# Moving a tile of w_out between the inverse transforms, and the prompt's spectrum and the gating to GpSimd

## The reference

```python
def _mixer(h, rows, s0, l, p):
    proj = h @ p['w_in'][l]                       # q, ff, fb, iv, g, hy
    ...
    o_hg = o.reshape(B, L, HG_WIDTH) * jax.nn.silu(g)          # 512 channels: gated scans
    v, x1, x2 = jnp.split(hyc, [HY_WIDTH, 2 * HY_WIDTH], axis=-1)
    u = x1 * v
    z = _long_conv(u, kern) + p['hy_d'][l] * u                 # by Fourier transforms
    y_hy = x2 * z                                              # 512 channels: Hyena
    y_hy = y_hy * lax.rsqrt(jnp.mean(y_hy * y_hy, -1) + EPS) * p['hy_norm_w'][l]
    out = jnp.concatenate([o_hg, y_hy], -1) @ p['w_out'][l]

def _layer(x, cvec, rows, s0, l, p):
    sh1, sc1, g1, sh2, sc2, g2 = ...              # from the conditioning vector
    x = x + g1 * mixer(rmsnorm(x) * (1 + sc1) + sh1)
    x = x + g2 * convffn(rmsnorm(x) * (1 + sc2) + sh2)
```

## Time and profile before

| what | value |
| --- | --- |
| median of three runs | 913.55 us |
| the profiled execution | 912.88 us |
| its span | 911.1 us |
| VectorE busy | 717.0 us, 79% |
| ScalarE busy | 443.3 us, 49% |
| GpSimd busy | 38.9 us, 4% |
| chain that ended last, by engine | TensorE 84%, VectorE 9%, ScalarE 3% |
| TensorE's mean granted clock | 0.996 of full speed |

### The profile page before, as it was taken

How to read it: one execution, slowest core, us unless ns; L and a number is a source line. 1 busy time by engine, 2 the same in 40 slices (tenths; PEclk the granted TensorE clock), 3 DMA queues, 4 the chain that set the end, 5 groups by cost and what they waited for, 6 DMA issues and landing times.

```text
span 911.1 us, 14075 instructions
## 1 busy us (share of the span) xinstructions
PE 887.6 (97%) x5374; PEld 788.7 (87%) x5374; DVE 717.0 (79%) x911; ACT 443.3 (49%) x710; POOL 38.9 (4%) x58
## 2 busy tenths in 40 slices
PE   7999999999999999999899999999999999999997
PEld 4479898898898898688779999999999999998885
DVE  5744755966966985699678899999999999988645
ACT  5745324334343323332276756556565656565443
POOL 2200000100000000002000000000000000000000
PEclk9999999999999999999999999999999999999999
DMA  8765233144134244325511232233313232345703
GB/s 297 244 217 174 83 126 138 37 157 145 63 122 145 91 164 137 89 70 112 144 46 48 76 131 99 97 110 114 115 62 130 108 111 88 131 152 202 261 0 116
DMA packets 39275, 112.76 MB, mean 124 GB/s; under 512 B 4471, under 2 KB 12663, under 8 KB 38568
## 3 DMA queue, kind: packets, MB, share of 16 engines
q1 hardware_dynamic: 33944, 93.58, 30.3%
q0 software_dynamic: 4800, 17.99, 6.5%
q10 hardware_dynamic: 464, 0.30, 0.1%
HBM read 101.48 MB, written 10.37 MB: 123 GB/s over the span
## 4 chain that ended last, share of the span: by engine, by line
PE 84%; DVE 9%; ACT 3%; issue 2%; DMA 1%; ACTq 0%; DVEq 0%; POOLq 0%
PE ps L2005 19%; PE ps L2006 19%; PE ps L2007 19%; PE ps L2505 14%; PE ps L2226 4%; PE ps L2025 2%; PE ps L2086 2%; PE ps L2238 1%; PE ps L2363 1%; DMA part<-in_rates 1%; DVE w_lo L1377 1%; PE ps L2033 1%; PE ps L2246 1%; DMA w<-in_hy_w 1%; ACT xn L1154 1%
## 5 line engine op out<-in xcount | busy, mean ns | idle before, releaser
L2005 PE MATMUL ps<-h_hi,w_hi 128*128 128x320 f32 x620 | 196.3, 317 | 2.8 <-DVE w_lo L1377 1.4
L2007 PE MATMUL ps<-h_hi,w_lo 128*128 128x320 f32 x620 | 191.6, 309 | 0.0
L2006 PE MATMUL ps<-h_lo,w_hi 128*128 128x320 f32 x620 | 191.5, 309 | 0.0
L2005 PEld LDWEIGHTS ps<-h_hi,w_hi 128*128 128x128 f32 x620 | 116.6, 188 | 4.1 <-issue 3.1
L2006 PEld LDWEIGHTS ps<-h_lo,w_hi 128*128 128x128 f32 x620 | 116.6, 188 | 0.0
L2007 PEld LDWEIGHTS ps<-h_hi,w_lo 128*128 128x128 f32 x620 | 116.4, 188 | 0.0
L1868 DVE TENSOR_TENSOR w_lo<-raw,w_hi 128x1024 fp32r<-128x1024 f32 (+1 forms) x53 | 64.2, 1212 | 18.6 <-ACT w_hi L1220 17.6
L1220 ACT ACTIVATE w_hi<-raw 128x1024 fp32r<-128x1024 f32 (+1 forms) x53 | 55.5, 1047 | 31.8 <-PE ps L2007 31.7
L1377 DVE TENSOR_TENSOR w_lo<-raw,w_hi 128x1024 fp32r<-128x1024 f32 x44 | 53.4, 1224 | 6.4 <-ACT w_hi L904 5.2
L2005 PE MATMUL ps<-w_hi,h_hi 128*128 128x512 f32 x120 | 49.6, 413 | 2.0 <-DVE h_lo L1734 2.0
L904 ACT ACTIVATE w_hi<-raw 128x1024 fp32r<-128x1024 f32 x44 | 45.8, 1057 | 4.4 <-DMA raw<-in_slots 2.4
(11 more groups left out here) (320 smaller groups left out, 2067.2 us busy)
## 6 DMA issues: line engine op xcount, KB each, us to landing
raw<-in_slots SPq DMA_DIRECT2D x138, 512.0 KB, 4.7
acts<-actf POOLq DMA_DIRECT2D x22, 320.0 KB, 2.5
raw<-in_slots SPq DMA_DIRECT2D x24, 256.0 KB, 6.5
xf<-acts SPq DMA_DIRECT2D x12, 320.0 KB, 6.6
wsum<-acts SPq DMA_DIRECT2D x10, 320.0 KB, 7.7
xin<-in_x_sample SPq DMA_DIRECT2D x4, 512.0 KB, 11.2
grow<-gates POOLq DMA_DIRECT2D x2, 1024.0 KB, 12.3
x<-in_x_sample POOLq DMA_DIRECT2D x2, 1024.0 KB, 13.7
```

The lines of the kernel that those rows point to most:

```text
L2005: mm(out, lhs[0], rhs[0], start=first, stop=False)
L2006: mm(out, lhs[0], rhs[1], start=False, stop=False)
L2007: return mm(out, lhs[1], rhs[0], start=False, stop=last)
```

## The change

- GpSimd does the prompt's spectrum (six multiplications, additions and subtractions of 128x512 and a copy) in place of VectorE. It signals `up_multiplied`, for which `z_prompt(0)` waits.
- GpSimd gates the raw tiles in place of VectorE, one by one, as ScalarE has taken them: ten instructions of 128x512 instead of four larger ones. The residual's DMAs stay behind them, on the same list.
- TensorE does nine raw tiles, then z_sample(0), z_prompt(0), z_sample(1), z_prompt(1), the tenth raw tile, and then the rest of the inverse transforms, each z_prompt right behind its z_sample.
- z has two buffers in turn, `zc` and `prod`.
- ScalarE makes y's upper parts (`square_y`), right ahead of the squares; VectorE waits for `y_upper` before the lower ones, and does those of channel block c behind the y of block c + 1.
- The last two units of the lower half of `w_out` are split later: on ScalarE behind the squares of blocks 1 and 2, on VectorE behind the last lower part of y.
- `mix` is called by halves: mix(0) and mix(1) for the first column half, then for the second.
- Some semaphores of the filter stage are merged: `taps_made` and `hid_made` become `filter_made`, `silu_in` and `bound_in` become `exp_in`, and so on, with the counts adapted.

```diff
@@ gpsimd
-            for n in range(2):
-                cols = slice(n * HW, (n + 1) * HW)
-                eng.wait_ge(sem("raw_gated"), n + 1)
+            eng.wait_ge(sem("up_ready"), 1)
+            r, t = sq[:, 0:HW], x1[:, 1, NT - 1, :]
+            G = nc.gpsimd.tensor_tensor
+            link(G(r, Up[:, 0, :], kspec_p[:, 0, :], ALU.mult))
+            link(G(t, Up[:, 1, :], kspec_p[:, 1, :], ALU.mult))
+            link(G(r, r, t, ALU.subtract))
+            link(G(t, Up[:, 0, :], kspec_p[:, 1, :], ALU.mult))
+            link(G(Up[:, 1, :], Up[:, 1, :], kspec_p[:, 0, :], ALU.mult))
+            link(G(Up[:, 1, :], Up[:, 1, :], t, ALU.add))
+            link(nc.gpsimd.tensor_copy(Up[:, 0, :], r), "up_multiplied")
+            eng.wait_ge(sem("ld_gate1"), 16)
+            for n in range(2):
+                cols = slice(n * HW, (n + 1) * HW)
+                for i in range(NT):
+                    eng.wait_ge(sem("raw_taken"), n * NT + i + 1)
+                    x = x1[:, n, i, :]
+                    nc.gpsimd.tensor_tensor(x, x, grow1[:, int(i == NT - 1), cols], ALU.mult).then_inc(sem("raw_gated"), 1)
+                eng.wait_ge(sem("raw_gated"), (n + 1) * NT)
                 eng.dma_start(x1[:, n, 0:NT - 1, :], ..., accum_op=ALU.add).then_inc(sem("ld_res"), 16)
...
@@ scalar
+            def take_raw(n, i):
+                eng.wait_ge(sem("hg_mixed"), n * NT + i + 1)
+                if n * NT + i == 2 * NT - 1:
+                    eng.wait_ge(sem("up_multiplied"), 1)
+                A(x1[:, n, i, :], ps[:, HG_BANKS[(n * NT + i) % 2], :], ACT.Copy).then_inc(sem("raw_taken"), 1)
...
+            def square_y(c):
+                w = v("hy_norm", c)
                 eng.wait_ge(sem("yhy_ready"), c + 1)
+                A(ap(h_hi, (NC + c) * T, [(GRID, ROWS), (1, GRID)]), grid(x2, c * CONV), ACT.Copy, scale=w)
+                A(h_hi[:, NC + c, TS:T], x2[:, c, PADS:CONV], ACT.Copy, scale=w).then_inc(sem("y_upper"), 1)
                 if c:
                     eng.wait_ge(sem("ysq_used"), c)
                 A(sq[:, 0:TS].rearrange("p (r c) -> p r c", c=GRID), grid(x2, c * CONV), ACT.Square)
                 A(sq[:, TS:T], x2[:, c, PADS:CONV], ACT.Square).then_inc(sem("ysq_ready"), 1)
+                if 0 < c < NC - 1:
+                    split_hi(UNIT_WOUT + 5 + c)
+
+            for c in range(NC):
+                eng.wait_ge(sem("z_made"), c + 1)
+                if c >= 2:
+                    eng.wait_ge(sem("yhy_ready"), c - 1)
...
+                if c == 1:
+                    take_raw(1, NT - 1)
+                if c:
+                    square_y(c - 1)
+            square_y(NC - 1)
@@ vector
             multiply(0)
             multiply(1)
-            eng.wait_ge(sem("up_ready"), 1)
-            r, t = prod[:, 0, 0, :], prod[:, 1, 0, :]
-            link(V.tensor_tensor(r, Up[:, 0, :], kspec_p[:, 0, :], ALU.mult))
...
-            link(V.tensor_copy(Up[:, 0, :], r), "zspec_ready")
...
-            gate_raw(0)
             for k in range(2):
                 split_lo(UNIT_WOUT + 4 + k)
-            gate_raw(1)
...
@@ in split_y
-                link(V.tensor_scalar(hi_lat, x_lat, w, None, ALU.mult))
-                link(V.tensor_scalar(hi_ctx, x_ctx, w, None, ALU.mult))
+                eng.wait_ge(sem("y_upper"), c + 1)
...
-                split_y(c)
-                if c < 2:
-                    split_lo(UNIT_WOUT + 6 + c)
+                if c:
+                    split_y(c - 1)
+            split_y(NC - 1)
+            for k in range(2):
+                split_lo(UNIT_WOUT + 6 + k)
@@ tensor
+            for at in range(2 * NT - 1):
+                raw_tile(*divmod(at, NT))
...
             z_sample(0)
+            z_prompt(0)
             z_sample(1)
-            z_prompt(0)
+            z_prompt(1)
+            raw_tile(1, NT - 1)
             z_sample(2)
-            z_prompt(1)
+            z_prompt(2)
             z_sample(3)
+            z_prompt(3)
             eng.wait_ge(sem("raw_taken"), 2 * NT)
             sum_channels(0)
-            z_prompt(2)
             sum_channels(1)
-            z_prompt(3)
...
-            mix(0)
-            mix(1)
+            mix(0, (0,))
+            sum_channels(3)
+            mix(1, (0,))
+            mix(0, (1,))
+            mix(1, (1,))
             mix(2)
```

More of the change, by code:

```diff
@@ L646, in build, with z_buffer @@
         V_BANKS = (0, 2, 3, 4, 1)
+        def z_buffer(c):
+            return ap(prod if c % 2 else zc, 0, [(1, T)])
         def ada_buffer(e):
@@ L1117, in _ @@
             for n in range(2):
[L1118 to L1134, removed]
+                for i in range(NT - n):
+                    take_raw(n, i)
+                if n == 0:
+                    for k in range(2):
+                        split_hi(UNIT_WOUT + 4 + k)
+            def square_y(c):
+                w = v("hy_norm", c)
                 eng.wait_ge(sem("yhy_ready"), c + 1)
+                A(ap(h_hi, (NC + c) * T, [(GRID, ROWS), (1, GRID)]), grid(x2, c * CONV), ACT.Copy, scale=w)
+                A(h_hi[:, NC + c, TS:T], x2[:, c, PADS:CONV], ACT.Copy, scale=w).then_inc(sem("y_upper"), 1)
                 if c:
@@ L1738, in _ @@
                 eng.wait_ge(sem("z_ready"), c + 1)
[L1739 to L1742, removed]
-                split_y(c)
-                if c < 2:
-                    split_lo(UNIT_WOUT + 6 + c)
+                z = z_buffer(c)
+                link(V.scalar_tensor_tensor(out=z, in0=u_hy[:, c, :], scalar=v("hy_d", c),
+                                            in1=z, op0=ALU.mult, op1=ALU.add))
+                link(V.tensor_tensor(grid(x2, c * CONV), grid(x2, c * CONV), rows64(z[:, 0:TS]), ALU.mult))
+                link(V.tensor_tensor(x2[:, c, PADS:CONV], x2[:, c, PADS:CONV], z[:, TS:T], ALU.mult), "yhy_ready")
+                if c:
+                    split_y(c - 1)
+            split_y(NC - 1)
+            for k in range(2):
+                split_lo(UNIT_WOUT + 6 + k)
             eng.wait_ge(sem("ysq_used"), NC)
@@ L2049, in tap_pair @@
                         if d:
-                            last.then_inc(sem("taps_made"), 1)
+                            last.then_inc(sem("filter_made"), 1)
             def tap_prompt():
@@ L2115, in _ @@
                 last = mm(ps[rows, 0, 0:SIDE], w2[rows, :], hid[rows, 0, :], start=True, stop=True)
-            last.then_inc(sem("hid_made"), 1)
+            last.then_inc(sem("filter_made"), 1)
             keep_busy(4)
@@ L2373, in _, with raw_tile @@
             eng.wait_ge(sem("heads_split"), 1)
-            for n in range(2):
+            def raw_tile(n, i):
                 units = [unit_ready(UNIT_WOUT + 2 * n + p) for p in range(2)]
[L2376 to L2382, removed]
-                        last = split_product(ps[:, HG_BANKS[at % 2], :], [x[:, k, i * P:(i + 1) * P] for x in (h_hi, h_lo)],
-                                             [w[:, k % 2 * HW:(k % 2 + 1) * HW] for w in units[k // 2]], k == 0, k == NC - 1)
-                    last.then_inc(sem("hg_mixed"), 1)
+                at = n * NT + i
+                if at == 0:
+                    eng.wait_ge(sem("uspec_ready"), 2)
+                if at >= 2:
+                    eng.wait_ge(sem("raw_taken"), at - 1)
+                for k in range(NC):
+                    last = split_product(ps[:, HG_BANKS[at % 2], :], [x[:, k, i * P:(i + 1) * P] for x in (h_hi, h_lo)],
+                                         [w[:, k % 2 * HW:(k % 2 + 1) * HW] for w in units[k // 2]], k == 0, k == NC - 1)
+                last.then_inc(sem("hg_mixed"), 1)
+            for at in range(2 * NT - 1):
+                raw_tile(*divmod(at, NT))
             def sum_channels(c):
@@ L2410, in z_prompt @@
                 if c == 0:
-                    eng.wait_ge(sem("zspec_ready"), 3)
+                    eng.wait_ge(sem("up_multiplied"), 1)
                 if c >= 2:
@@ L2420, in _ @@
             z_sample(0)
+            z_prompt(0)
             z_sample(1)
-            z_prompt(0)
+            z_prompt(1)
+            raw_tile(1, NT - 1)
             z_sample(2)
-            z_prompt(1)
+            z_prompt(2)
             z_sample(3)
+            z_prompt(3)
             eng.wait_ge(sem("raw_taken"), 2 * NT)
             sum_channels(0)
-            z_prompt(2)
             sum_channels(1)
-            z_prompt(3)
-            units = [unit_ready(UNIT_WOUT + 4 + p) for p in range(4)]
             def mix(i, ns=(0, 1)):
-                order = [(n, k) for n in ns for k in range(NC, KD)]
-                if i == 0:
-                    order.sort(key=lambda step: step[1])
-                for n, k in order:
+                units = {n: [unit_ready(UNIT_WOUT + 4 + 2 * n + p) for p in range(2)] for n in ns}
+                for n, k in [(n, k) for n in ns for k in range(NC, KD)]:
                     if i == 0 and n == 0:
@@ L2446, in mix @@
```

(4 more changed lines are left out.)

59 lines of the change are left out of this document (27 added, 32 removed).

## The result

| | median | ratio to the kernel before |
| --- | --- | --- |
| before, beside it | 914.25 us | |
| after | 935.31 us (934.71 to 935.48) | 1.0226 [1.0203, 1.025] |

The kernel is slower, as forecast, but by 21.1 us where 14.4 were forecast; 935.31 lies 3.3 us above the 932 up to which the forecast's range reached. The profiled execution took 935.43 us, its span is 933.6 against 911.1, so 22.5 us are to be found between the two traces. TensorE's mean granted clock is 0.984 of full speed, before it was 0.996.

What follows compares the result with a forecast made beforehand. TensorE, busy for 97% of the 911.1 us span, bounds the kernel; 13.0 us of idle TensorE, 1.7 of half clock and a net -0.3 gave +14.4 us, 927.3 (about 927.5 beside the median), with 923 to 931 as range, 919 to 932 with rivals.

Steps and rivals of the forecast that it cites:

- four waits: TensorE's waits around the inverse transforms: 1.09 (z's copy), 0.43 (squares), 0.49 and 1.46 us (y's lower part).
- two overlaps: Two cases in the trace before where a GpSimd and a VectorE operation meet and one waits out the other.
- first rival: No hindrance: VectorE's multiply keeps its pace, only gaps are rearranged; 911.5 to 913.5 us, say 912.5; chance 0.16.
- second rival: GpSimd starves: VectorE never hands over, z_prompt(0) waits 6.2 us for the prompt's spectrum; +8.6 us, 922; chance 0.10.
- z_sample(0) late: First inverse transform on TensorE waits for VectorE's lengthened multiply, starting at 425.6 instead of 412.58: 13.0 us idle.
- half clock in z_sample(0): After the long gap TensorE's clock is at 0.50 and the first 4 us of z lose 1.7 us.
- sum 0 to the second mixed tile: TensorE from the first channel sum through mix(1): gain 1.9 us, clock drop charged 1.6, net -0.3 us.
- With both always pending they alternate: VectorE's multiply and GpSimd's operations take turns: a pair takes 2.20 us instead of 1.26, each GpSimd operation costing 0.94.
- slower still: Rival: hand-overs at full length in multiply, each GpSimd operation costing VectorE 1.24 us, 18.9 instead of 14.4; 932 us; chance 0.04.
- bound of 15.1: Upper bound beside the 13.0 us of idle TensorE, if GpSimd's copy costs as much as its other operations.
- two clock charges: TensorE's half clock: 1.7 us in the first z_sample, 1.6 us behind the wait after sum 1.
- new wait: TensorE stands 2.4 us for y's third lower part, S + 4.8 to S + 7.2, S being sum 0's start.

Runs made afterwards that it cites:

- e7: The kernel before with only GpSimd's two shares (prompt's spectrum, gating) moved there, old order of TensorE and ScalarE, a few semaphores merged: 932.09 us, ratio 1.0195.
- e9: e6 with fifteen linked GpSimd memsets of 128x512, which only write, beside multiply, results unused: 908.28 us, one run.
- e10: e6 with fifteen linked GpSimd copies of 128x512 from SBUF beside multiply, results unused: 911.99 us, one run.
- e8: The changed kernel with the residual's first two DMAs issued behind the ninth gating instead of the fifth, gatings still unlinked: 932.61 us, ratio 1.0202.
- e5: The changed kernel with unused products of ones by ones on TensorE, sixty in the long gap, ten in the short one: 929.96 us, ratio 1.0173.
- e6: e4 with mix taking the second tile's first two channel blocks ahead of the first tile's third: 908.64 us, ratio 0.994.
- e1: The changed kernel with GpSimd's shares (prompt's spectrum, gating) back on VectorE, all else as changed: 916.36 us, ratio 1.0024.
- e4: e1 with sum_channels(0) ahead of z_sample(3) instead of behind z_prompt(3): 911.95 us, ratio 0.9981.
- e11: The kernel before with only the merged and renamed filter-stage semaphores, and GpSimd's additions there linked as after: 913.4 us, ratio 0.9998.
- e2: The changed kernel with GpSimd waiting for the end of each gating before issuing the next: 933.02 us, ratio 1.0212.
- e3: The changed kernel with GpSimd's gatings started only when multiply(1) has ended, prompt's spectrum still beside multiply: 923.75 us, ratio 1.011.

## What the prediction had right, and where it failed

*The bound, the mechanism and the sign: right.* The size was not: +14.4 forecast, +22.5 between the profiled runs, +21.1 between the medians. All four rows of the table below fell short. (Of the 5.8 us that could be won, the forecast's four waits and the 1.6 of the clock make only 5.1; nothing hangs on the rest.) The forecast rested on two overlaps and the rule read from them, that the later operation starts 0.15 before the other's end. It held for twelve of the sixteen GpSimd operations that meet `multiply` (0.97 to 0.99 each against 0.94, the very first 1.1; the copy 0.29 against 0.3). The first rival, no hindrance, fell in the changed kernel and in e7. GpSimd did not starve, its operations took 2.15 each; the second rival fell too.

The Trainium skill, SBUF - State Buffer, section Who interferes with whom, says that an instruction of VectorE with two SBUF inputs contends with a GpSimd instruction that reads SBUF, and not with one that only writes it. The trace agrees: e9 has 1.22 a row beside writes, e10 1.51 beside copies. The same section says that order of issue decides which of the two is blocked; by that rule VectorE's instruction, whose record begins 0.59 us before the first of the four gatings, should have gone first. It took 7.47 us, so the recorded starts and the rule don't agree here, and the measurement decides.

The terms against what was measured:

| term | forecast | measured | from |
| --- | --- | --- | --- |
| z_sample(0) late | 13.0 | 16.1 | 430.09 - 1.45 - 412.58 |
| half clock in z_sample(0) | 1.7 | 2.7 | 6.15 - 3.46 |
| sum 0 to the second mixed tile | -0.3 | 2.7 | 24.1 instead of 21.1 |
| late before the stage | 0 | 1.45 | 391.70 - 390.25 |
| sum | 14.4 | 22.9 | the spans: 22.5 |

The remaining 0.4 is mostly the 0.28 between the 452.4 that the forecast took for mix(1)'s end and the 452.68 at which VectorE's second `mix_tile` starts.

*"With both always pending they alternate": the first step that failed.* It held until GpSimd's first DMAs. The gatings are not linked, and the next four were pending behind two DMA issues. They ran in a row, and VectorE's instruction took 7.47 instead of 1.22, so 6.25 more or 1.56 for each gating (the 0.59 before the first of them included) instead of 0.94: 2.5 us of the 3.1 that the first term is short, the other 0.5 being the 0.03 to 0.05 by which each alternation was dearer, and the first's 0.17. e8, where all alternate, has `multiply` 14.9 us longer, against 14.4 forecast. The "slower still" rival priced a full hand-over for every operation, 932; what came was more than that, but for four of them only. The bound of 15.1 beside the 13.0 was not one for the gap: it is 16 times 0.94, the lengthening of `multiply`, from which the 1.45 of slack has still to be taken; for the gap it would have been 13.7, and 16.1 came.

*The two clock charges: the second step that failed, and the larger one.* I charged 1.7 and 1.6, the price of the one stretch in the trace, both times with a reason (the gap was longer) that spoke for more. They measured 2.7 and about 4.3 (24.1 less 0.28 less the 19.5 that the path has at full clock by the forecast), 3.7 us more than charged. In the first stretch the clock stayed at 1.2 GHz for 5.3 us of work behind the gap (430.09 to 435.4); in the second it fell 1.1 us behind the wait (458.23 to 459.3) and stayed there for 10.2 us. e5 gives 5.4 of these 7.0 back by keeping TensorE busy, and e6 runs without a drop in that stage. The bound of 1.9 to 2.0 for each came from a single stretch, and should not have been an upper bound.

*The new wait: right.* Forecast from S + 4.8 to S + 7.2; in the changed kernel and in e1 y's lower part comes at S + 7.1, and the wait is 2.26. That its path runs through ScalarE's squares, which wait for sum 0, is borne out by e4. That the order of TensorE and ScalarE alone gains 0.3 was not: e1 is at 1.0024 [1.0008, 1.0041], 2 us slower. The clock behind this wait takes the gain, as e4 and the one run of e1 at 912.57 indicate.

*At nothing.* The merged semaphores were rightly costed at 0 (e11), though the 1.45 us ahead of the stage stay without a cause; the residual too: its last DMAs are issued from 445.8 on, and `mix_tile(0)` at 472.5 waits for TensorE, not for them.

What stays open is why the instruction that VectorE issued at 415.83 in the changed kernel had to wait for gatings that began at 416.42 and after, while the one at 415.89 in e2, with the same DMA issues beside it, went through in 1.22. The records don't show when GpSimd's instructions ask for their inputs, and why gatings that follow a DMA issue run in a row is not shown either. Nor was it tried to take GpSimd's gating off `multiply` altogether and off z too, for instance by letting it work from PSUM.

## What to carry to other kernels

Before work is moved from VectorE to GpSimd, look at what VectorE does at that time: if its instructions have two inputs in SBUF, each GpSimd instruction that reads SBUF is added to VectorE's time, here 0.97 us of a two-input operation of 1.28 and 0.29 of a copy. Here instructions that had stood behind the multiply on VectorE's list opened no gap there (e1), and cost 17.4 us within it, where TensorE waits for its last result. Unlinked GpSimd instructions that pile up behind a DMA issue were worse than linked ones. A wait of TensorE among one-column products can cost less than the clock behind it (here 2.26 us, and 10.2 us at half clock): fill it with products of another tile that are ready (e6, 5.5 us under the kernel before), or with empty ones.

## What the runs showed of the hardware

- VectorE's two-input operation of 1.22 us beside GpSimd's of 128x512: 1.22 beside a write of 0.58, 1.51 beside a copy, 2.20 beside an operation of two inputs. Beside GpSimd issuing a DMA with accumulation: 1.22.
- GpSimd's pending, unlinked multiplications ran four or five in a row behind a DMA issue, and one VectorE instruction took 7.47 (the changed kernel), 8.12 (e3) and 8.69 us (e7).
- A wait of 2.26 us between one-column products was followed by 10.2 us at 1.2 GHz, one of 1.32 to 1.46 by 3.4 us, in the same place (the changed kernel and e1; before and e4). After an idle gap of 2.99 us the clock had fallen (e10); after one of 15.9 us the clock rose 5.3 us behind the first product (430.09 to 435.4).
